# Dense products in reversed column order, with the gated tiles 64 bytes further apart

## The reference, cut to what matters

```python
# first block
y = parallel_mixer(rmsnorm(x, norm_mix_pre), w_in, ..., w_out)
x = x + rmsnorm(y, norm_mix_post)
y = memory_cross_attention(rmsnorm(x, norm_mem_pre), rmsnorm(mem, mem_norm_g), w_mem_q, w_mem_kv, w_mem_o)
x = x + rmsnorm(y, norm_mem_post)
u = dwconv_centred(rmsnorm(x, norm_ffn_pre) @ w_up, ffn_dw, ffn_dw_b)
x = x + rmsnorm((gelu(u[..., :D_FF]) * u[..., D_FF:]) @ w_down, norm_ffn_post)
# second block, i = 0 and 1; swiglu(h) = (silu(h @ w_gate) * (h @ w_up)) @ w_down
x = x + 0.5 * swiglu(rmsnorm(x), ...)
x = x + (pool_mixer(rmsnorm(x), ...) if i == 0 else mla_mixer(rmsnorm(x), ...))
x = x + 0.5 * swiglu(rmsnorm(x), ...)
```

## Time and profile before

| what | value |
|---|---|
| median of 3 runs | 2583.47 us (2579.31 to 2584.01) |
| the profiled execution | 2585.77 us, its span 2584.5 us |
| TensorE products busy | 2540.1 us, 98% of the span, 11694 products |
| VectorE, ScalarE, GpSimd busy | 1218.3, 933.2, 615.6 us |
| mean granted TensorE clock | 0.989 of full speed |
| DMA | 227.28 MB, mean 88 GB/s |

### The profile page before, as it was taken

How to read it: one execution, slowest core, us unless ns; L and a number is a source line. 1 busy time by engine, 2 the same in 40 slices (tenths; PEclk the granted TensorE clock), 3 DMA queues, 4 the chain that set the end, 5 groups by cost and what they waited for, 6 DMA issues and landing times.

```text
span 2584.5 us, 28793 instructions
## 1 busy us (share of the span) xinstructions
PE 2540.1 (98%) x11694; PEld 2087.8 (81%) x11694; DVE 1218.3 (47%) x1611; ACT 933.2 (36%) x1372; POOL 615.6 (24%) x469
## 2 busy tenths in 40 slices
PE   8999999999999999999999999999999999999999
PEld 7777777788887888888888888888888787888887
DVE  5896565555635333335333333333336566433332
ACT  4486343344423333224332222223224454423321
POOL 3663302222203222111222111222101431222200
PEclk9999999999999999999999999999999999999999
DMA  4211312333232233222323333333232111233332
GB/s 169 74 42 57 98 41 66 98 98 98 92 98 79 91 98 95 95 92 81 103 95 97 93 97 96 98 98 96 90 100 79 48 44 47 93 98 98 96 98 92
DMA packets 66484, 227.28 MB, mean 88 GB/s; under 512 B 7216, under 2 KB 8752, under 8 KB 66352
## 3 DMA queue, kind: packets, MB, share of 16 engines
q1 hardware_dynamic: 66352, 225.44, 27.7%
HBM read 223.31 MB, written 2.10 MB: 87 GB/s over the span
## 4 chain that ended last, share of the span: by engine, by line
PE 92%; DVE 4%; ACT 2%; issue 1%; POOL 0%; DMA 0%; SPq 0%; DVEq 0%; ACTq 0%; POOLq 0%
PE main L384 20%; PE main L386 19%; PE main L385 19%; PE score L384 7%; PE score L386 6%; PE score L385 6%; PE out L384 3%; PE out L385 3%; PE out L386 3%; DVE wl L376 1%; PE main L2017 1%; DVE tmp L1331 1%; PE turn L454 0%; PE turn L453 0%; PE turn L1011 0%
## 5 line engine op out<-in xcount | busy, mean ns | idle before, releaser
L376 DVE TENSOR_TENSOR wl<-raw,wh 128x1024 fp32r<-128x1024 f32 (+1 forms) x431 | 561.9, 1305 | 806.4 <-ACT wh L368 805.5
L368 ACT ACTIVATE wh<-raw 128x1024 fp32r<-128x1024 f32 (+1 forms) x431 | 439.9, 1024 | 609.6 <-PE main L386 490.0
L384 PE MATMUL main<-hxh,wh 128*128 128x512 f32 x1208 | 475.8, 394 | 7.7 <-DVE tmp L671 4.2
L386 PE MATMUL main<-hxh,wl 128*128 128x512 f32 x1208 | 472.4, 391 | 0.0
L385 PE MATMUL main<-hxl,wh 128*128 128x512 f32 x1208 | 472.3, 391 | 0.0
L384 PE MATMUL main<-hh,wh 128*128 128x512 f32 x880 | 342.6, 389 | 1.9 <-POOL hl L1572 0.9
L385 PE MATMUL main<-hl,wh 128*128 128x512 f32 x880 | 342.4, 389 | 0.0
L386 PE MATMUL main<-hh,wl 128*128 128x512 f32 x880 | 342.3, 389 | 0.0
L384 PEld LDWEIGHTS main<-hxh,wh 128*128 128x128 f32 x1208 | 228.3, 189 | 60.4 <-DVE tmp L671 4.3
L384 PE MATMUL score<-hxh,wh 128*128 128x512 f32 x664 | 261.3, 394 | 6.4 <-DVE wl L376 4.8
L386 PEld LDWEIGHTS main<-hxh,wl 128*128 128x128 f32 x1208 | 228.1, 189 | 48.0
(11 more groups left out here) (424 smaller groups left out, 3425.7 us busy)
## 6 DMA issues: line engine op xcount, KB each, us to landing
raw<-in_wts SPq DMA_DIRECT2D x375, 512.0 KB, 3.6
raw<-in_wts SPq DMA_DIRECT2D x52, 384.0 KB, 3.1
x<-in_xT SPq DMA_DIRECT2D x4, 512.0 KB, 8.2
out<-x SPq DMA_DIRECT2D x8, 256.0 KB, 3.9
memx<-in_memT SPq DMA_DIRECT2D x1, 1024.0 KB, 9.6
raw<-in_wts SPq DMA_DIRECT2D x4, 256.0 KB, 2.6
band<-in_pool SPq DMA_DIRECT2D x1, 768.0 KB, 4.4
rope<-in_rope SPq DMA_DIRECT2D x1, 512.0 KB, 7.1
```

The costliest lines, as they stand in the source:

```text
L368: e.activation(wh[i % NCONV][:, 0:n], raw[i % NRAW][:, 0:n], ACT.Copy).then_inc(*sig.up("weight_high", ("high", i)))
L376: e.tensor_tensor(wl[i % NCONV][:, 0:n], raw[i % NRAW][:, 0:n], f(wh[i % NCONV][:, 0:n]), ALU.subtract) \
L384: e.matmul(o, ah, bh, start=start, stop=False)
L386: return e.matmul(o, al, bh, start=False, stop=stop)
```

## The change: what it does

In `linear` and `pair_step` the moving operands and the output are written with a step of -1: column 511 of the moving tile is the first to enter and its result goes to column 511 of the bank, then 510, and so on. What is computed is the same, column by column. The rows of `hh` and `hl` become 528 elements (2112 bytes), of which 512 are used; the writers and readers name columns 0 to 512.

```diff
-        hh, hl = new("hh", [P, FT, S], F32R), new("hl", [P, FT, S], F32R)
+        hh, hl = new("hh", [P, FT, S + 16], F32R), new("hl", [P, FT, S + 16], F32R)
...
-                made = mm3(e, o, (h[:, k, :], lo[:, k, :]), (sh, sl), first and k == 0, last and k == nk - 1)
+                made = mm3(e, o[:, ::-1], (h[:, k, :], lo[:, k, :]), (sh[:, ::-1], sl[:, ::-1]), first and k == 0, last and k == nk - 1)
...
-                made = mm3(e, o, (h[:, k, :], lo[:, k, :]), (sh, sl), k == 0, k == KC - 1)
+                made = mm3(e, o[:, ::-1], (h[:, k, :], lo[:, k, :]), (sh[:, ::-1], sl[:, ::-1]), k == 0, k == KC - 1)
...
-            return lambda k: (hh[:, k, :], hl[:, k, :], ("h", nm, k))
+            return lambda k: (hh[:, k, 0:S], hl[:, k, 0:S], ("h", nm, k))
```

More of the change, by code:

```diff
@@ L1532, in conv_ffn_scalar @@
                     e.wait_ge(*sig.at(("yn", "mempost", KC - 1)))
-                    e.activation(hh[:, c, :], tile_turn.of(("tile", n - 6, "s"))[:, :], ACT.Copy).then_inc(*sig.up("h_high", ("hh", "ffn", c)))
+                    e.activation(hh[:, c, 0:S], tile_turn.of(("tile", n - 6, "s"))[:, :], ACT.Copy).then_inc(*sig.up("h_high", ("hh", "ffn", c)))
         def conv_ffn_vector(e):
@@ L1571, in conv_ffn_gpsimd @@
                 e.wait_ge(*sig.at(("hh", "ffn", c)))
-                e.tensor_tensor(hl[:, c, :], s1[:, :], f(hh[:, c, :]), ALU.subtract).then_inc(*sig.up("h_low", ("h", "ffn", c), ("free", ("tile", 2 * c, "s"))))
+                e.tensor_tensor(hl[:, c, 0:S], s1[:, :], f(hh[:, c, 0:S]), ALU.subtract).then_inc(*sig.up("h_low", ("h", "ffn", c), ("free", ("tile", 2 * c, "s"))))
         half_turn = Ring(tmp_slots)
@@ L1609, in gated_scalar @@
             e.wait_ge(*sig.at(ended))
-            e.activation(hh[:, c, :], s[:, :], ACT.Copy).then_inc(*sig.up("h_high", ("hh", nm, c)))
+            e.activation(hh[:, c, 0:S], s[:, :], ACT.Copy).then_inc(*sig.up("h_high", ("hh", nm, c)))
         def gated_vector(e, nm, u, c):
@@ L1673, in swiglu_gpsimd @@
                 e.wait_ge(*sig.at(("hh", nm, c)))
-                e.tensor_tensor(hl[:, c, :], s1[:, :], f(hh[:, c, :]), ALU.subtract).then_inc(*sig.up("h_low", ("h", nm, c), ("free", (nm, "gs", c))))
+                e.tensor_tensor(hl[:, c, 0:S], s1[:, :], f(hh[:, c, 0:S]), ALU.subtract).then_inc(*sig.up("h_low", ("h", nm, c), ("free", (nm, "gs", c))))
             if next_nm:
```

## The result

| | before | after |
|---|---|---|
| median | 2583.3 us (2579.31 to 2584.01) | 2633.81 us (2632.68 to 2639.38) |
| span of the profiled execution | 2584.5 us | 2633.4 us |
| mean granted TensorE clock | 0.989 | 0.994 |

The ratio after to before is 1.0205, 95% interval 1.0189 to 1.0222. The forecast was 2583.5 us within 2570 to 2625; the time lies above that range.

What follows compares the result with a forecast made beforehand. TensorE, busy 98% of the span, was taken as the bound: number of products times the step between starts. The profiled 2585.8 us + 0 + 0 + 0, adjusted to the median of the runs, gave 2583.5 us, range 2570 to 2625.

Steps and rivals of the forecast that it cites:

- No instruction added, consumers unmoved: Whole kernel: same products, semaphores, waits and DMAs, and consumers wait for the whole accumulation; cost 0.
- The pad: 64 extra bytes per row of hh and hl: only shifts what lies behind; cost 0, bounds -1 and +1 us.
- the comparison of `hh` with `hxh`: Dense products moving hh or hxh both take 389 ns with the same step, so spacing was said not to matter.
- The reversed read: Moving operand of the products in linear and pair_step: a step of -1 stays with its neighbour; cost taken as zero.
- the gapped 256-column operand: L384 score<-wh,ckh, gathered from two runs with a gap: 0.120 us a step, like one run, so unusual reads cost nothing.
- The prediction's other argument for a free read: SBUF lines of 16 bytes need two hits; a descending read of 4-byte elements has four, so reading costs nothing.
- The reversed write: Output to PSUM in linear and pair_step: no earlier row shows a descending write, so the rows are silent; cost taken as zero.
- The surcharge of 13.7 ns: Time between two TensorE products, 226.7 against 213 ns: a fixed sum per product, not per column, kept under reversal.
- Rival C: Dense products: reversed order sheds the surcharge from products meeting at a bank's end; 127 us less, 2457 us, chance 0.03 in full.
- Rival A: Dense products: full rate only for ascending pairs, 0.431 instead of 0.2267 us each, 4476 us; chance 0.17.
- Rival B: Dense products: fixed start cost at the far end of bank or tile, up to 4.1 ns each, 2590 to 2622 us; chance 0.09.
- the prediction's own list of signs: Records in 100 us of pure products: 443 step kept, about 233 one column per tick, 433 start cost, 470 surcharge shed.

Runs made afterwards that it cites:

- e7: Kernel before, ascending, gated tiles of each network shifted together: down-product step 226.7 ns at 512 bytes, 226.8 at 256, 228.9 at 64, 233.3 at 128.
- e13: Kernel before, ascending, with hxh, hxl and all weight buffers 64 bytes up, hh and hl not: step 226.7 ns gate and up, 233.3 down.
- e9: Kernel before, no pad, another column order per stage for read and write alike: 430 or 431 records for walks down over 128 columns or more, otherwise 443.
- e3: Kernel before with only the moving operand read in reverse, result written ascending, no pad: 2636.77 us, ratio 1.0216.
- e4: Kernel before with only the result written in reverse, moving operand read ascending, no pad: 2581.49 us, ratio 0.9998.
- e8: Kernel before, ascending, with the weight buffers wh and wl 64 bytes further up: 2638.48 us against 2583.32, step 233.3 ns in every network.
- e14: Kernel before, ascending, with only the low weights wl 64 bytes up: mean step 231.1 ns; the three steps of a triple 228.3, 229.2 and 235.8.
- e16: Kernel before, ascending, down products' hl alone, both, or hh alone shifted by 192 bytes: mean steps 228.9, 233.3 and 234.4 ns.
- e15: Kernel before, ascending, wl placed ahead of wh and only wh 64 bytes up: mean step 231.1 to 231.5 ns in some networks, 233.3 in others.

## Why the prediction was wrong, point by point

**What bounds the kernel.** Right. TensorE's step times its number is the time: 9192 x 6.67 ns, less what fewer half-clock stretches gave back, is the whole difference to within 1 us, and no other engine took part.

**No instruction added, consumers unmoved.** Right; the waits of TensorE are those of before.

**The pad, "cost 0, bounds -1 and +1 us".** Wrong: 11.5 us alone. The step that failed is the comparison of `hh` with `hxh`. By the kernel's map both lay at multiples of 2048 bytes from the weight buffers, so by e7 and e13 the rows compared two places that are the same place. They could say nothing on a third. Inside the change the pad costs nothing visible, since the reversed read is already at 233.3 ns (2633.81 against 2633.42 us); why the reversed read with mixed distances isn't slower than that, when single distances give 236.7, I did not find out.

**The reversed read, "I take zero".** This is the step that failed, and the term of the sum that was mis-sized: 6.67 ns a product, 61.3 us where the sum has 0. It rested on a step of -1 staying with its neighbour and on the gapped 256-column operand. That row goes up like every other, and e9 shows that swapped halves and quarters and blocks of 4 read downwards are free while a long walk down is not. Only the walk down was the question, and no row of before had one. The prediction's other argument for a free read falls with e3, in which the read alone is reversed and costs the 6.67 ns. Besides, at 256 columns the effect has the other sign.

**The reversed write.** Right: 0.9998, and the rows were silent on it.

**The surcharge of 13.7 ns, "I keep it".** Wrong in the reading. It seemed fixed because 512 and 256 columns showed it alike. It is 13.3 ns at distance 0 ascending (226.67 - 213.33), 20 descending, and for 256 columns, which take 106.7 ns by themselves (half of their 213.4 at a granted clock of 0.50), 13.3 ascending, 11.7 descending and as low as 6.7 with the weights 64 bytes up: it depends on direction, width and distance to the weights. A hint lay in the timeline with the weight loads (PEld) in it, here of the changed kernel:

```profile
2300.06 0.40 PE L384 MATMUL score<-hxh,wh 128*128 128x512 f32 x1
2300.07 0.19 PEld L385 LDWEIGHTS score<-hxl,wh 128*128 128x128 f32 x1
2300.29 0.40 PE L385 MATMUL score<-hxl,wh 128*128 128x512 f32 x1
```

Each load starts together with the product before the one it serves, so two reads of SBUF run side by side in every step. Rival C asked the right question, whether the surcharge depends on the order. It looked for the place in the PSUM bank, where e4 finds nothing, and had the wrong sign for 512 columns.

**Rival A** (one column per slow tick, 4476 us) fell. The Trainium skill's "PSUM — Partial Sum Buffer", section Specifications, by which any non-contiguous pattern slows matmuls significantly, does not reach a step of -1: the measured write costs nothing.

**Rival B** came nearest in size (at most 4.1 ns a product, 2622 us; it was 6.67, less what the clock gave back), by luck, as its cause is wrong. Its start cost at the far end is refuted by the swapped halves and quarters. By the prediction's own list of signs 430 records would have been read as B (433). The range ended with B at 2625 us, 9 us short; its end came from the largest step seen in a stretch just after a pause, while single steps of 231 to 236 ns were to be found in the same trace.

**What is shown and what is argued.** Shown: the read side alone carries it; moving the weights alone does the same; moving both together undoes it; for tiles shifted together the pattern repeats after 256 bytes; both the reversal and the moved weights cost nothing at half the clock (426.7 ns in the after trace and in e8). Argued: that the two reads, the moving tile's and the weight load's, get into each other's way in SBUF. It fits the runs that move tiles or weights as a whole; its simplest form, in which a product pays for the load beside it, does not fit e14 and e16, and no run took the load out from beside a product. The Trainium skill's "TensorE: Matmul & The Clock Gate", section "Part 2: What happens when you issue a matmul", says that there are two independent read ports and that loading the next tile's weights doesn't steal read bandwidth from the running matmul. By that rule 64 bytes between tile and weights would cost nothing; here they cost 2.2 or 6.7 ns of 226.7, depending on which way, and the measurement decides. Open: which load counts for a product, why one placement can run in two rhythms (e15), why 256 columns have the opposite sign, and why `hh` alone is worse than `hh` and `hl` together.

None of the placements or orders beat the kernel before for 512 columns, so no further version was run. The 256-column products of `linear` would gain 1.7 ns each descending and at most 6.7 ns with other weights' places, but there are 192 of them: 0.3 and 1.3 us.

## What to carry to other kernels

Where TensorE is busy for 98% of the time, measure the step between starts, not the duration, and ask of each layout or order change what it does to the two reads that run in every step. For streams of 512-column float32r products with a weight load each, as here, start with moving tiles and weight buffers at a distance that is a multiple of 256 bytes, and read tiles upwards; padding tiles apart "to be safe" cost 0.54%. With 256 columns both rules had the opposite sign, so measure for the width at hand. And a comparison of two groups proves independence of a property only if the two groups differ in it.

## What I had not expected of the hardware

- 64 bytes under the weight buffers (one run each): 2638.48 against 2583.32 us.
- The same 64 bytes took 256-column products from 120.0 to as low as 113.3 ns.
- The same descending order costs 6.67 ns with 512 columns and saves 1.67 ns with 256.
- 512 columns, all gated tiles shifted together, by the bytes of the shift. Ascending, 0, 256 or 512: 226.7 ns; 64: 228.9; 32, 96, 128, 192, 384: 233.3; 160: 234.3. Descending: 0, 64, 192, 256: 233.3; 128, 384: 236.7.
- At a granted clock of 0.50 the step is 426.7 ns in both orders and with the weights moved.
